# Side work regrouped in one expert loop, and a layer's tail put in another order

## The reference

```
sh_m, sc_m, g_m, sh_f, sc_f, g_f = adaln(c, ada_w[l], ada_b[l])        # silu(c) @ ada_w + ada_b, six parts
x = layer_norm(DEEPNORM_ALPHA * x + g_m * mixer(modulate(x, sh_m, sc_m)))
x = layer_norm(DEEPNORM_ALPHA * x + g_f * moe(modulate(x, sh_f, sc_f)))

moe:  gates = sigmoid scores of the 6 chosen of 64 experts, normalised, times 2.5
      hidden = silu(t @ w_gate[e]) * (t @ w_up[e])                     # 1024 -> 128 for each expert
      out = sum over e of (hidden * gates[:, e]) @ w_down[e] + shared expert

s5:   u = h @ w_in_c                                                   # 64 groups of 16 channels
      state[t] = lam_bar * state[t-1] + b_bar u[t]  (64 complex states a group, forward and backward)
      y = Re(C state_fwd) + Re(C state_bwd) + d * u
      z = gelu(y) @ w_out_c;  out = z_val * sigmoid(z_gate)
```

## Time and profile before

| what | us |
| --- | --- |
| three runs | 1615.79, 1618.09 (median), 1621.24 |
| the profiled execution's own time | 1615.59 |
| its span | 1613.5 |
| layer 0 mixer and start of its mixture | 0 to 252 |
| first mixture in steady state (PE busy all of it) | 252 to 810 |
| end of first mixture, norm | 810 to 841 |
| S5 layer | 841 to 1027 |
| second mixture | 1027 to 1613 |

### The profile page before, as it was taken

The page is one execution under the profiler, slowest core; times in us unless marked ns, Lnnn a source line. Parts: engine busy times, 40 slices in busy tenths (PEclk is TensorE's granted clock), DMA queues, the critical chain, the costliest instruction groups (busy, mean ns, idle before and its releaser), DMA issues. The chain is left out here.

```text
span 1613.5 us, 26749 instructions
## 1 busy us (share of the span) xinstructions
PE 1435.9 (89%) x10938; PEld 1295.5 (80%) x10938; DVE 1040.7 (64%) x1535; ACT 588.1 (36%) x685; POOL 34.1 (2%) x37
## 2 busy tenths in 40 slices
PE   5887679999999999999958459399999999999995
PEld 1866668888888888888947359399999999999995
DVE  7535467777777887887873723765656565656565
ACT  2434243333333333333322633443333334333432
POOL 2000100000000000000010000100000000000001
PEclk8979789999999999999978669799999999999998
DMA  9663459999999887888655996065555555555540
GB/s 364 247 226 117 149 161 342 327 323 317 328 328 325 301 284 267 274 289 289 237 175 210 193 292 221 35 232 204 209 198 191 205 209 198 192 206 208 197 145 26
DMA packets 155592, 372.83 MB, mean 231 GB/s; under 512 B 19160, under 2 KB 74744, under 8 KB 153216
## 3 DMA queue, kind: packets, MB, share of 16 engines
q1 hardware_dynamic: 155520, 371.88, 68.4%
HBM read 349.21 MB, written 21.50 MB: 230 GB/s over the span
## 5 line engine op out<-in xcount | busy, mean ns | idle before, releaser
L267 PE MATMUL PS<-moe_mod_HThl,moe_up_h 128*128 128x256 f32 x2080 | 595.4, 286 | 2.8 <-DVE moe_up_l L1559 2.8
L269 PE MATMUL PS<-moe_mod_HThl,moe_up_l 128*128 128x256 f32 x2080 | 589.3, 283 | 0.0
L268 PE MATMUL PS<-moe_mod_HThl,moe_up_h 128*128 128x256 f32 x2080 | 589.1, 283 | 0.0
L267 PEld LDWEIGHTS PS<-moe_mod_HThl,moe_up_h 128*128 128x128 f32 x2080 | 399.2, 192 | 27.3 <-issue 24.7
L268 PEld LDWEIGHTS PS<-moe_mod_HThl,moe_up_h 128*128 128x128 f32 x2080 | 399.3, 192 | 2.5
L269 PEld LDWEIGHTS PS<-moe_mod_HThl,moe_up_l 128*128 128x128 f32 x2080 | 399.2, 192 | 0.0
L1559 DVE TENSOR_TENSOR moe_up_l<-raw,moe_up_h 128x2048 fp32r<-128x2048 f32 x130 | 297.3, 2287 | 41.3 <-ACT moe_up_h L1548 41.3
L1564 DVE TENSOR_TENSOR moe_down_l<-raw,moe_down_h 128x1024 fp32r<-128x1024 f32 x130 | 159.2, 1225 | 198.1 <-ACT moe_down_h L1552 198.1
L1548 ACT ACTIVATE moe_up_h<-raw 128x2048 fp32r<-128x2048 f32 x130 | 247.0, 1900 | 15.4 <-PEq L1231 6.6
L1552 ACT ACTIVATE moe_down_h<-raw 128x1024 fp32r<-128x1024 f32 x130 | 137.7, 1059 | 292.9 <-PE PS L269 292.9
L267 PE MATMUL PS<-moe_down_h,moe_hid_h 128*128 128x512 f32 x520 | 204.3, 393 | 2.7 <-DVE moe_hid_l L1695 2.7
(11 more groups left out here) (364 smaller groups left out, 1412.7 us busy)
## 6 DMA issues: line engine op xcount, KB each, us to landing
raw<-in_exp_w_gate SPq DMA_DIRECT2D x128, 512.0 KB, 3.9
raw<-in_exp_w_up SPq DMA_DIRECT2D x128, 512.0 KB, 5.1
raw<-in_exp_w_down SPq DMA_DIRECT2D x128, 512.0 KB, 6.0
side_slices<-in_ada_w SPq DMA_DIRECT2D x56, 512.0 KB, 7.1
moe_gate_b<-gate_rows SPq DMA_DIRECT2D x128, 128.0 KB, 3.7
part_slices<-in_ada_w SPq DMA_DIRECT2D x18, 512.0 KB, 6.9
raw<-in_ada_w SPq DMA_DIRECT2D x8, 1024.0 KB, 11.3
G<-in_s_bt SPq DMA_DIRECT2D x32, 256.0 KB
```

The costliest lines, as they stand in the source:

```text
L267: pe.matmul(out, ah, bh, start=start, stop=False, skip_group_check=True)
L268: pe.matmul(out, ah, bl, start=False, stop=False, skip_group_check=True)
L269: return pe.matmul(out, al, bh, start=False, stop=stop, skip_group_check=True)
```

## The change

The 56 conditioning slices are no longer multiplied one an item: in items 6, 10, 14, 18, 22, 26, 30 and 33 four at once, and in every second item from 35 on two at once, beside the taps. The 32 into-state pieces stand in items 4 to 30, with two pieces each in items 8, 13, 18, 23 and 28 (`E_ITEMS`), the 32 from-state halves in items 31 to 62, one each; the last taps come in item 63. The first two loads of `S5Build` move on SP from ahead of the gate rows to behind the weights of item 2's visit (`load(2)`). In both mixtures PE transposes the gates ahead of `down(0)`. In the S5 layer the within-chunk matrices get memory of their own and are loaded by 16 transfers on GpSimd's queue, 8 after half of the second block of the first product is ready and 8 after u is turned; the from-state matrices are loaded into `raw` as the z product frees it; the end state's transpose stands ahead of the from-state products; ACT's and DVE's lists around the last product are reordered, the high copy of gelu's result goes from ACT to DVE, and the last product takes its first half of k from the first half of gelu's result.

```diff
+    def used_at(self, m):
+        n, y = divmod(m, SIDE)
+        if n < TAPS_GROUP - 1:
+            return FIRST + SIDE * n + (3 if y < RING else 7)
+        if n == TAPS_GROUP - 1:
+            return FIRST + SIDE * n + (3 if y < RING else 6)
+        return FIRST + SIDE * n + y // 2 * 2
     def sync(self, sp, i):
-        m = i - FIRST - 2
-        if RING <= m < N_SIDE * SIDE:
-            sp.wait_ge(part_used, SIDE * W_SIDE + m - RING + 1)
-            self.load(sp, m)
+        for m in range(RING, N_SIDE * SIDE):
+            late = 1 if m - RING < TAPS_GROUP * SIDE and m % RING >= 2 else 0
+            if self.used_at(m - RING) + 5 + late == i:
+                sp.wait_ge(part_used, SIDE * W_SIDE + m - RING + 1)
+                self.load(sp, m)
         n, step = divmod(i - FIRST - SIDE - 6, SIDE)
...
-    FIRST_E, FIRST_F, AHEAD = 1, 33, 5
+    FIRST_F, AHEAD = 31, 5
+    E_ITEMS = sorted(list(range(4, 31)) + [8, 13, 18, 23, 28])
     def __init__(self, scope):
         mem = G[:, :, :, :].rearrange("p a r d -> p (a r d)")
     def halves(self, i):
         f = i - self.FIRST_F
-        return [f] if 0 <= f < 30 else [30, 31] if f == 30 else []
+        return [f] if 0 <= f < 32 else []
+    def pieces(self, i):
+        return [e for e in range(32) if self.E_ITEMS[e] == i]
         done = i - self.AHEAD
-        e = done - self.FIRST_E
-        if 0 <= e < 32:
+        for e in self.pieces(done):
             sp.wait_ge(self.e_built, e + 1)
             sp.dma_start(et_d[:, e // 2, e % 2 * 512:e % 2 * 512 + 512], self.ET[e % 2]).then_inc(self.e_stored[e % 2], 16)
             if e + 2 < 32:
                 self.load_e(sp, e + 2)
-            if e == 28:
+            if e == 27:
                 self.load_f(sp, 0)
-        if e == 31:
-            sp.wait_ge(self.e_stored[0], 16 * 16)
+        if done == self.FIRST_F:
+            for b in range(2):
+                sp.wait_ge(self.e_stored[b], 16 * 16)
             self.load_b(sp, 0)
-        if e == 32:
-            sp.wait_ge(self.e_stored[1], 16 * 16)
             self.load_f(sp, 1)
...
+        wait(dve, self.e_built, e)
     def vector(self, dve, i):
-        e = i - self.FIRST_E
-        if 0 <= e < 32:
+        for e in self.pieces(i):
             self.into_state(dve, e)
...
                         side.first(sp)
-                        s5.first(sp)
                     sp.wait_ge(s["gatesT"], 1)
+                        if side and i == 2:
+                            s5.first(sp)
...
                     up(1, 1)
-                    down(0, 0, first=True)
                     pe.wait_ge(s["gates"], 2)
                     for r in range(REQ):
                         mm = pe.transpose(PS[0:NE, 2, r * TOK:(r + 1) * TOK], gt[:, r, :], ident)
                     mm.then_inc(s["gates_turned"], 1)
+                    down(0, 0, first=True)
                     for i in range(2, FIRST):
...
-                                        s5.tensor(pe, it * SIDE + (x + 2 - lo * SIDE), it * (SIDE // 2) + (x // 2 + 1 - lo * SIDE // 2), x // 2 % 2)
+                    with pe.Fori(0, TAPS_GROUP - 1) as it:
+                        group(it, 0)
+                    for x in range(SIDE):
+                        i = (TAPS_GROUP - 1) * SIDE + FIRST + x
+                        both(i, i % 2)
+                        if side:
+                            for y in side.slices_at(TAPS_GROUP - 1, x):
+                                side.tensor(pe, TAPS_GROUP - 1, y)
+                            if i == taps_at:
+                                s5.tensor(pe, 2, 1, 0)
+                    with pe.Fori(TAPS_GROUP, N_SIDE) as it:
...
-        VF = sb("s5_rows_or_from", [P, 8 * 1024], F32, scope)
+        V = sb("s5_rows", [P, 2048], F32, scope)
+        MF = sb("s5_inside", [P, 3 * 2048], F32, scope)
...
                 into(3)
                 rows(2)
                 rows(3)
-                sp.wait_ge(u_mm, 4)
-                for n in range(2):
-                    sp.dma_start(VF[:, 4096 * n:4096 * n + 4096].rearrange("p (a x) -> p a x", a=4), f_d[:, 4 * n:4 * n + 4, :]).then_inc(f_landed[n], 16)
+                for j in range(RING):
+                    sp.wait_ge(z_mm, (3 * j + 2) // 2 + 1)
+                    sp.dma_start(raw[j][:, :].rearrange("p (a x) -> p a x", a=3), f_d[:, 3 * j:3 * j + 3, :]).then_inc(f_landed[j], 16)
                 sp.wait_ge(z_mm, 8)
-                for n, (lo, hi) in enumerate(((0, 6), (6, 12), (12, 16))):
-                    out = raw[n][:, 0:512 * (hi - lo)]
-                    for s in range(CH):
-                        src = kt_d[:, 4 * lo:4 * hi, (CH - 1 - s) * C5:(CH - 1 - s) * C5 + P]
-                        sp.dma_start(out[s * C5:(s + 1) * C5, :].rearrange("c (g x) -> c g x", x=P), src).then_inc(m_landed[n], 16)
-                sp.dma_start(N1[:, :].rearrange("p (a x) -> p a x", a=4), f_d[:, 8:12, :]).then_inc(f_landed[2], 16)
-                sp.dma_start(raw[2][:, 2048:3072], f_d[:, 12, :]).then_inc(f_landed[3], 16)
-                sp.dma_start(raw[3][:, :].rearrange("p (a x) -> p a x", a=3), f_d[:, 13:16, :]).then_inc(f_landed[3], 16)
+                sp.dma_start(N1[:, :].rearrange("p (a x) -> p a x", a=4), f_d[:, 12:16, :]).then_inc(f_landed[4], 16)
                 sp.wait_ge(in_mm, 1)
-                for j in range(3):
+                norm.sync(sp)
+                for j in range(RING):
+                    sp.wait_ge(y_mm, 3 * j + 3)
                     w_out.load(sp, j)
-                sp.wait_ge(y_mm, 4)
-                w_out.load(sp, 3)
...
                 for a in range(NAT):
-                    if a in (0, 6, 12):
-                        pe.wait_ge(m_landed[a // 6], 16 * CH)
+                    if a in (0, 12):
+                        pe.wait_ge(m_landed[a // 12], 16 * CH)
                     for q in range(4):
                         mm = pe.matmul(y_at(a, q), U[:, a, q, :], inside_matrix(a)[:, q * P:(q + 1) * P], start=(a % 4 == 0), stop=False,
                                        skip_group_check=True)
                 mm.then_inc(in_mm, 1)
+                pe.wait_ge(ends, 1)
+                pe.transpose(PS[:, 7, 0:P], HS[:, :], ident).then_inc(end_t, 1)
                 pe.wait_ge(xn_ready, 2 * NC5)
                 for a in range(NAT):
-                    if a % 4 == 0:
-                        pe.wait_ge(f_landed[a // 4], 16 if a < 12 else 32)
+                    if a % 3 == 0:
+                        pe.wait_ge(f_landed[a // 3 if a < 12 else 4], 16)
                     f = ft(a)
                     for i in range(2):
                         for q in range(4):
                             at = ((a * 2 + i) * 4 + q) * RJ
                             mm = pe.matmul(y_at(a, q), XN[:, at:at + RJ], f[:, (2 * q + i) * P:(2 * q + i + 1) * P], start=False,
                                            stop=(i == 1 and a % 4 == 3), skip_group_check=True)
-                    if a % 4 == 3:
-                        mm.then_inc(y_mm, 1)
-                pe.wait_ge(ends, 1)
-                pe.transpose(PS[:, 7, 0:P], HS[:, :], ident).then_inc(end_t, 1)
+                    mm.then_inc(y_mm, 1)
+                pe.wait_ge(end_s, 1)
                 for half in range(2):
                     for e in range(2):
                         pe.wait_ge(yv[e], half + 1)
...
-                act.wait_ge(ends, 1)
-                w_out.high(act, 0)
-                for b in (0, 2):
-                    act.wait_ge(y_mm, b + 1)
-                    y_rows(copy, b).then_inc(yv[0], 1)
                 act.wait_ge(end_t, 1)
                 copy(HSt[:, :], PS[:, 7, 0:P]).then_inc(end_s, 1)
+                for b in (0, 2):
+                    act.wait_ge(y_mm, 4 * b + 4)
+                    y_rows(copy, b).then_inc(yv[0], 1)
...
+                pool.wait_ge(w_in.ready[0], 2)
+                for n, (home, lo, hi) in enumerate(((MF, 0, 12), (V, 12, 16))):
+                    if n:
+                        pool.wait_ge(u_mm, 4)
+                    for s in range(CH):
+                        src = kt_d[:, 4 * lo:4 * hi, (CH - 1 - s) * C5:(CH - 1 - s) * C5 + P]
+                        pool.dma_start(home[s * C5:(s + 1) * C5, :].rearrange("c (g x) -> c g x", x=P), src).then_inc(m_landed[n], 16)
...
-                w_out.low(dve, 0)
                 for b in (1, 3):
-                    dve.wait_ge(y_mm, b + 1)
+                    dve.wait_ge(y_mm, 4 * b + 4)
                     y_rows(copy, b).then_inc(yv[1], 1)
+                    if b == 1:
+                        w_out.low(dve, 0)
                 for half in range(2):
+                    dve.wait_ge(gelu, 4 * half + 4)
+                    at = slice(half, KD, 2)
+                    copy(mod.h[:, at, :], Gf[:, at, :]).then_inc(g_hi, 1)
                     dve.wait_ge(g_hi, half + 1)
-                    at = slice(half, KD, 2)
```

102 lines of the change are left out of this document (52 added, 50 removed).

## The result

The changed kernel takes 1683.85 us (median of four runs, 1683.35 to 1688.99) against 1616.94 of the kernel before: a ratio of 1.0417, 95% interval 1.0387 to 1.0448. Slower was forecast, but 15 us and not 67. The profiled execution is the slowest of the four, with a span of 1687.2 against 1613.5, so the 73.7 us that are shared out here are 7 more than the medians differ by.

A forecast was written before the change was run, and what follows sets the result against it. It took PE's list to bound the first mixture and a chain of waiting steps the S5 layer. Gains of −30.2 us and +45 for the doubles gave net +15, so 1632 us, range 1601 to 1664 (the forecast's own 1618 to 1650).

The forecast's parts named there:

- F: First mixture, items with two pieces: the second piece's load is issued too late, five doubles cost +45 us.
- E: S5 tail: from-state products start earlier and the last product starts at about 950 to 951, not 962.08: −11 us.
- A: First mixture: items with side work on PE go from 60 to 23, 0.34 us saved a visit: −12.2 us.
- B: First mixture: gates ahead of down(0), first piece loads behind load(2), so up(3) starts earlier and warm: −3.1 us.
- C: Second mixture: gates' transposes ahead of down(0) shorten DVE's 4.26 us wait for the gate row: −1.8 us.
- D: Tail of the mixture: one half an item and taps in item 63 cut waits for the last half: −2.1 us.
- L1 + L2 − 5.3: Lateness of a double from its two loads' issue-to-landing times, put at 8.0 and 7.0 us: 9.7 us a double.
- Rival 1: Doubles' loads land early, L 5 us or less, as the queue has emptied: 1593 to 1606 us; chance 0.24.
- Rival 3: S5 tail gains nothing, as GpSimd's small packets slow u's rows and z: sum +26, 1643 us; chance 0.14.
- Rival 2: Bandwidth: items 4 to 30 want 350 GB/s, each late by up to 0.7 us: 1655 to 1670 us; chance 0.14.

The follow-up runs named there:

- a_single: The changed kernel with pieces one an item, as in the kernel before; grouped slices, gates and S5 layer stay changed: 1622.9 us, ratio 1.0019.
- best3: best2 with the S5 layer of the kernel before: 1607.1 us, ratio 0.9936.
- best4: best3 with the compute order of the changed S5 tail, transfers as before: 1601.5 us, ratio 0.9915.
- b_doubles5: The kernel before with the changed kernel's list of pieces (items 4 to 30, five doubles), slices one an item: 1666.7 us, ratio 1.0316.
- a_ahead4: The changed kernel with S5Build's step on SP one visit earlier (AHEAD = 4 for 5): 1633.1 us, ratio 1.0085.
- a_inside_late: The changed kernel with all 16 within-chunk transfers, still on GpSimd, waiting until u is turned: 1684.8 us, ratio 1.0399.
- s5_spread: a_single with the within-chunk transfers, still on GpSimd, spread into gaps between u's rows, the rest once u is turned: 1614.9 us, ratio 0.9982.
- s5_spread_late: s5_spread with SP's four from-state loads into raw held until the z product is done: 1613.4 us, ratio 0.9970.
- s5_inside_sp: a_single with the within-chunk transfers issued by SP instead of GpSimd, at the same points: 1626.0 us, ratio 1.0060.
- best1: a_single with the S5 order of b_s5_after_z and item 33's slices loaded a visit earlier: 1608.1 us, ratio 0.9945.
- best2: best1 with S5Build's step one visit earlier (AHEAD = 4): 1606.3 us, ratio 0.9929.
- b_s5_after_z: The kernel before with the changed S5 layer, 14 of 16 within-chunk transfers only after the z product: 1616.7 us, ratio 1.0000.
- a_s5before: The changed kernel with the S5 layer of the kernel before; mixtures stay changed: 1675.1 us, ratio 1.0345.

## Why the prediction was wrong

Between the forecast's +15 and the 73.7 of the profiles lie 59 us: 31 of them are F's and 27.5 are E's.

**A, fewer visits (−12.2).** Right. Two items from 35 on took 9.70 + 9.26 and now 10.03 + 8.60, 0.33 less for one visit less. −4.9 stand in the table behind `up(34)`, and 22 visits by 0.34, 7.5 us, are inside the +68.4. Whether they come out depends on the loads: from `up(4)` to `up(34)` a_single took 278.6 us, no less than the 278.0 of before, and only best3 and best4 got down to 271.6 and 272.1.

**B, C, D (−3.1, −1.8, −2.1).** Right within 0.5 in size: −3.5, −2.1 (the gate's wait went from 4.26 to 2.92) and −2.6. The causes are less sure. b_doubles5 gained 3.4 in B's stretch with the gates' transposes in their old place and pieces from item 4 on, a_single 4.6 with the transposes moved and pieces from item 1 on, so either alone brings as much as both. And a_single gained 2.0 of D's 2.6 with two halves in the last item and the taps behind it, as before; what D named is worth 0.6.

**F, the doubles (+45).** The mechanism is as foretold, item by item, and a_ahead4 and b_doubles5 show it; the size was off. Measured are 68.4 + 7.5 = 76: 70 at the five doubles, 3.6 at item 33, where DVE waits 6.2 us for the first from-state load, whose cost I had put at 0 to 2, and the rest in item 4 (1.5) and two slices more. The formula held: L1 + L2 − 5.3 a double, less 4 x 2.06, gives 51 us of idle with the measured loads, and PE's idle is 53, of which 2.3 are of the single piece in item 12.

What failed are the terms put into it. The first load of a double was put at 8.0, since "the queue empties", and took 9.2 to 11.2, 10.0 on the mean; the second, put at 7.0, took 5.8 to 8.0, 7.2 on the mean. That is 11 us too little. The restart at the lower clock was put at 1 us a double: 70 − 53 leaves 17 us, 3.3 a double or 2.1 for each of the eight restarts at 1.2 GHz, 12 too little. The load of before, 11.56 us, was not the upper end either: 15.5 in the changed kernel. b_doubles5, with slices one an item, came to 49, near the 45.

The Trainium skill ("DMA: Bandwidth & Descriptors", "Anatomy of one DMA — SWDGE (gpsimd) path") gives 2.0 us plus bytes/436e3, an estimate of 3.8 us for a trio. The trace doesn't agree: no load of a double that DVE waited for took under 5.8 us. Rival 1 was out by these loads.

**E, the S5 layer (−11).** The step that failed is "1.5 us I add for u's row copies and z, which now share the engines with the 16 transfers". It cost 22.3 us of waiting for rows (23.9 against 1.6), 5.2 in z, and 29.0 in all. The tail's own gain was under-estimated, 14.0 for 11. The number was in hand: 28 us of within-chunk transfers at a share of 1.23 leave nothing for a transfer behind them, and the row copies were put among three quarters of them. I priced a full queue as if it shared itself fairly with a small, urgent transfer. Rival 3 named this very mechanism, but let it only eat the gain: its price should have been the time of the packets ahead of the rows, over 20 us, and the sum +35. The Trainium skill's rule that transfers share the same 16 DMA engines whichever engine issued them ("DMA: Bandwidth & Descriptors", "Issuing engines are not separate DMA queues") agrees with the runs (27.6 us of waiting for rows with these transfers on SP's queue, 24.7 on GpSimd's); I had cited it and drawn only half of it.

**The sum.** Put right by what was measured: −12.4 − 3.5 − 2.1 − 2.6 + 76 + 16.5 (S5 layer without D) + 1.9 of a later start come to 73.8, the spans' difference of 73.7. It is the table put in the prediction's terms, and no second proof of them.

**Rival 2** (bandwidth) gave a time of 1655 to 1670 by another way: the share fell from 0.99 to 0.85, and a_ahead4 got 51 us back with the same bytes. Items away from the doubles kept 8.50 us, 8.60 behind a visit and 10.46 with four slices, so its lateness in each item didn't happen. Its load of 10 us for a double did.

**Open.** What PE waits for in z is argued, not shown. The idle is 5.2, 3.7, 9.1, 8.3, 8.1 and 4.0 us where most within-chunk transfers ran during z or just ahead of it (the changed kernel, a_single, a_inside_late, s5_spread, s5_spread_late, s5_inside_sp), and 2.1, 1.0 and 0 where two of them had gone out before z (best1, best2, b_s5_after_z). But it is 0.6, 1.6 and 1.3 in a_s5before, best3 and best4 as well, where none had, and in a_single the last of them moved 1.4 us before the idle began, so they can't be all of it. For instruction fetch speaks that in eight of these traces a 16 KB instruction transfer starts within the idle or less than 1 us ahead of it, and PE goes on 2.3 to 3.3 us after that start; no run changed it alone.

## What to carry to other kernels

When two uses of a double-buffered load are put into one step, look at where the load is issued, not at how long the work is: here 2 us of added work cost 10 to 14, since the issue hung on the very step that wanted the data. Price a queue by what stands ahead of the transfer that the critical path needs, in the time that those transfers were measured to take and not by their bytes at the rate of large loads; a second issuing engine changed nothing in that here. And give an idle of some microseconds on PE the lower clock behind it as well.

## What the runs showed of the hardware

The within-chunk transfers (rows of 512 bytes, into 16 partitions each) moved 4.2 MB in 33 us in the kernel before, where windows show 118 to 135 GB/s, and went at 111 to 114 GB/s from GpSimd's queue (b_s5_after_z from 910 to 930, the changed kernel from 935 to 945), all at a DMA share over 1.0. Large loads reached 422 GB/s (984 to 1000 us of the changed kernel). Whether the short rows or the 16 partitions make them slow wasn't tested. PE's restarts at the 1.2 GHz level, behind eight of the eleven idles at the doubles, cost 2.1 us each beside the idle (70 us lost at the doubles, 53 of them idle). And PE can stand still in the midst of a dense run of small matmuls with no semaphore to wait for, for up to 9.1 us (a_inside_late), while transfers fill the DMA engines.
